# One key projection for two heads of the latent attention, and weight splits over the valid tiles alone

## The chip, the core and the metric

The kernel runs on one core of a Trainium2 chip. The core has a matrix engine (PE, with its own queue for weight loads, PEld), a vector engine (DVE), a scalar engine (ACT), a general engine (POOL) and a sync engine (SP) that issues the loads here. Each engine works through its own instructions in order, and the engines wait for each other by semaphores. The metric is the device time of one execution in microseconds (us), less is better.

## What is computed

Two network blocks run one after the other on 512 tokens of width 1024. The change touches one part of the second block, its latent attention with 8 heads: a query of 64 plain and 32 rotary columns for each head, a key of 64 plain columns for each head, and one rotary key for all heads. In the reference, shortened:

```python
def mla_attention(c_q, c_kv, k_rope_raw, cos, sin, q_norm_g, w_uq, kv_norm_g, w_ukv, w_mla_out):
    q = rms_norm_2(c_q, q_norm_g) @ w_uq                      # 384 -> 8 heads x (64 + 32)
    q_nope, q_rope = q[..., :QK_NOPE], q[..., QK_NOPE:]
    q_rope = apply_rope(q_rope, cos, sin)
    kv = rms_norm_2(c_kv, kv_norm_g) @ w_ukv                  # 256 -> 8 heads x (64 + 64)
    k_nope, v = kv[..., :QK_NOPE], kv[..., QK_NOPE:]
    k_rope = apply_rope(k_rope_raw, cos, sin)
    ...
        s = einsum("bqhd,bkhd->bhqk", qn_b, k_nope) + einsum("bqhr,bkr->bhqk", qr_b, k_rope)
        p = softmax(where(mask, s, neg))
        return einsum("bhqk,bkhd->bqhd", p, v)
```

Beside it stand a convolution of 31 taps with a layer norm, and gates of both branches.

## The kernel before

Every product in full precision is made of three matmuls: a weight is split into a high and a low part (`split`: ACT writes `whi` from `raw`, DVE writes `wlo` as the rest), an input likewise, and high by high, high by low and low by high are summed. Activations are held with features on the 128 partitions and the 512 tokens along the free axis. Weights arrive by units of up to eight 128-column tiles in a ring of four buffers; SP loads a unit into `raw`, ACT and DVE split it three units ahead of its use, and PE's last matmul of a unit counts up `s_used`, which frees the buffer. `split` works on all 1024 columns, also where a unit has fewer.

The latent attention is a loop of 18 steps (`SLOTS`), written out for each engine; the order is the program's, there is no planner. Head h has two steps, 2h and 2h + 1, for two pairs of query blocks. In step s PE does this:

1. the scores of step s (`mla_scores`, L1147 to L1152),
2. a fill unit, 24 matmuls of the input projection (`in_unit`, L774 to L776): into `bank[1]` in even steps, into `bank[0]` in odd ones,
3. the product of probabilities and values of step s - 2 (`mla_pv`),
4. in even steps, the query projection of head s/2 + 1 (`project(h, "q")`, L1128 to L1130, nine matmuls) into `bank[0]`,
5. the transposes of the probabilities of step s - 1 (`mla_turn`, L1166),
6. in even steps, the key projection of the same head (`project(h, "k")`, six matmuls) into `bank[1]`.

A key projection yields 128 rows, 64 of key and 64 of value; the value rows aren't used, since all values are made in a unit of their own before the loop. Head 0 is projected before the loop, its key into `psT`.

The query of head h is taken out of `bank[0]` by two engines: ACT copies the 64 plain rows (L1913), DVE multiplies the 64 rotary rows by the table `rope` (`head_rope`, L2729), both into `tmp[0]`. Then ACT writes the high part `q2h` (L1916) and DVE the low part `q2l` (L2734). The key is split in place: ACT writes `k2h` (L1921), DVE `k2l` (L2740); the rotary key lies in rows 64 to 127 of both buffers already. The fill unit of an odd step waits until both readers of `bank[0]` are done (`h_cp`, `h_rp`); the fill unit of an even step waits for the low part of the key that was in `bank[1]` (`h_lo`).

DVE in step s: the row maxima of the scores (L2834), the split of a fill unit's weights (L2266), the reciprocals (L2850), its share of the convolution taps (L2716, L2721, four in most steps), the eviction of the fill unit (L2690; before the taps in steps 4 and 6), the attention output of step s - 2 (L2877, L2880), in even steps the rope step, the split of a head unit's weights and `q2l`, then the low part of the transposed probabilities (`pt2l`, L2893), and last, in even steps, `k2l`. ACT makes exponentials (L1981) and tap products (L1891) that POOL adds (L3352); POOL also scales the probabilities (L3370). After the taps, step 12 ends with PE's sums for the layer norm (L1116), whose mean DVE takes in step 13 (L2829).

## Time and profile before

| | us |
|---|---|
| median of 3 runs (2504.86 to 2504.95) | 2504.87 |
| profiled execution | 2504.7 |
| its span, first to last instruction | 2502.9 |
| PE busy in the span | 2488.7 (99%) |
| DVE busy | 1991.0 (80%) |
| ACT busy | 1244.7 (50%) |
| POOL busy | 305.5 (12%) |

A row of a timeline gives the start in us from the span's start, the length, engine, line, operation, what is written from what, shapes, and in brackets the idle time of the engine before it with what ended that. PE's matmuls overlap, so their lengths say less than the distances between their starts. A row of the table of waits gives who waited for whom, the total, the number and the longest.

### The profile page before, as it was taken

The page shows a single profiled execution, that of the slowest core. Times are in us where ns is not written, and L with a number is a line of the kernel's source. Part 1 is how long each engine was busy: PE and PEld are TensorE (multiplying, and loading weights), DVE is VectorE, ACT ScalarE, POOL GpSimd, SP SyncE. Part 2 cuts the span into 40 slices and gives each one's busy share as a digit, 9 for nine tenths or more (in the row PEclk, how much of TensorE's full clock was granted, in tenths as well). Part 3 has the DMA queues.
Part 4 walks back from the last instruction along what each step waited for, and adds up shares of the span by engine and source line. Part 5 has one row for each costly group of instructions (what it writes and reads, how often), then busy time and mean ns, then how long its engine had stood idle before and what let it go on. Part 6 is the DMA issues. An engine that isn't in the chain of part 4 may idle for free.

```text
span 2502.9 us, 36450 instructions
## 1 busy us (share of the span) xinstructions
PE 2488.7 (99%) x14212; PEld 2186.1 (87%) x14212; DVE 1991.0 (80%) x2830; ACT 1244.7 (50%) x1975; POOL 305.5 (12%) x250
## 2 busy tenths in 40 slices
PE   9999999999999999999999999999999999999998
PEld 7999988889999889999888899998888888888887
DVE  7878867778888688887777888876899786788873
ACT  6444444444444454444553544445577535654542
POOL 4000001320000000000023100000187221200002
PEclk9999999999999999999999999999999999999999
DMA  5333332223333323334323233334322333233331
GB/s 158 98 96 100 100 104 84 81 86 101 97 105 105 115 83 102 98 101 119 101 61 93 78 104 99 110 103 136 91 71 77 126 92 112 85 106 105 99 100 59
DMA packets 487297, 246.83 MB, mean 99 GB/s; under 512 B 42321, under 2 KB 483926, under 8 KB 486870
## 3 DMA queue, kind: packets, MB, share of 16 engines
q1 hardware_dynamic: 486674, 244.19, 33.9%
q8 instruction: 113, 1.85, 0.3%
q14 instruction: 58, 0.48, 0.1%
q10 hardware_dynamic: 452, 0.32, 0.0%
HBM read 240.27 MB, written 4.19 MB: 98 GB/s over the span
## 4 chain that ended last, share of the span: by engine, by line
PE 96%; DVE 2%; ACT 1%; DMA 0%; issue 0%; POOL 0%; DVEq 0%; ACTq 0%
PE bank L893 8%; PE bank L892 8%; PE bank L891 8%; PE bank L774 6%; PE bank L775 6%; PE bank L776 6%; PE psS L913 5%; PE psS L914 4%; PE psS L915 4%; PE bank L1454 3%; PE psT L957 2%; PE psT L959 2%; PE psT L958 2%; PE psT L774 2%; PE psT L775 2%; PE psT L776 2%
## 5 line engine op out<-in xcount | busy, mean ns | idle before, releaser
L2266 DVE TENSOR_TENSOR wlo<-raw,whi 128x1024 fp32r<-128x1024 f32 (+2 forms) x212 | 288.8, 1364 | 49.2 <-ACT whi L1581 46.0
L774 PE MATMUL bank<-xhl,whi 128*128 128x512 f32 x672 | 264.5, 394 | 0.0
L775 PE MATMUL bank<-xhl,whi 128*128 128x512 f32 x672 | 261.9, 390 | 0.0
L776 PE MATMUL bank<-xhl,wlo 128*128 128x512 f32 x672 | 261.8, 390 | 0.0
L891 PE MATMUL bank<-xshl,whi 128*128 128x256 f32 x840 | 237.8, 283 | 0.0
L892 PE MATMUL bank<-xshl,whi 128*128 128x256 f32 x840 | 237.7, 283 | 0.0
L893 PE MATMUL bank<-xshl,wlo 128*128 128x256 f32 x840 | 237.7, 283 | 0.0
L1581 ACT ACTIVATE whi<-raw 128x1024 fp32r<-128x1024 f32 (+2 forms) x209 | 214.4, 1029 | 37.3 <-PE bank L776 22.0
L2329 DVE TENSOR_TENSOR wlo<-tw,whi 128x1024 fp32r<-128x1024 f32 x140 | 171.6, 1226 | 62.5 <-ACT whi L1621 62.3
L913 PE MATMUL psS<-hhi,whi 128*128 128x512 f32 x488 | 191.7, 393 | 0.0
L914 PE MATMUL psS<-hlo,whi 128*128 128x512 f32 x488 | 191.6, 393 | 0.0
L915 PE MATMUL psS<-hhi,wlo 128*128 128x512 f32 x488 | 189.8, 389 | 0.0
L1621 ACT ACTIVATE whi<-tw 128x1024 fp32r<-128x1024 f32 x140 | 148.1, 1058 | 70.6 <-PE bank L893 56.4
L3258 POOL TENSOR_TENSOR sc<-sc,st 128x1024 f32<-128x1024 f32 (+1 forms) x16 | 27.0, 1685 | 1137.4 <-DVE st L2537 1137.4
L892 PEld LDWEIGHTS bank<-xshl,whi 128*128 128x128 f32 x840 | 161.3, 192 | 0.0
L893 PEld LDWEIGHTS bank<-xshl,wlo 128*128 128x128 f32 x840 | 161.3, 192 | 0.0
L891 PEld LDWEIGHTS bank<-xshl,whi 128*128 128x128 f32 x840 | 161.3, 192 | 0.0
L776 PEld LDWEIGHTS bank<-xhl,wlo 128*128 128x128 f32 x672 | 126.1, 188 | 26.7
L774 PEld LDWEIGHTS bank<-xhl,whi 128*128 128x128 f32 x672 | 126.2, 188 | 26.5 <-issue 1.1
L775 PEld LDWEIGHTS bank<-xhl,whi 128*128 128x128 f32 x672 | 126.3, 188 | 26.1 <-issue 1.0
L1685 ACT ACTIVATE hhi<-tmp 128x512 fp32r<-128x512 f32 x74 | 46.8, 633 | 141.8 <-DVE tmp L2455 138.8
L1628 ACT ACTIVATE whi<-raw 128x384 fp32r<-128x384 f32 (+2 forms) x140 | 79.6, 569 | 74.5 <-PE psS L915 74.1
(703 smaller groups left out, 7184.7 us busy)
## 6 DMA issues: line engine op xcount, KB each, us to landing
raw<-in_ffn_wg SPq DMA_DIRECT2D x88, 512.0 KB
raw<-in_ffn_wu SPq DMA_DIRECT2D x88, 512.0 KB
raw<-in_w_in SPq DMA_DIRECT2D x53, 512.0 KB
raw<-in_w_mlp SPq DMA_DIRECT2D x40, 512.0 KB
raw<-in_ffn_wd SPq DMA_DIRECT2D x48, 256.0 KB
raw<-in_ffn_wd SPq DMA_DIRECT2D x24, 448.0 KB
raw<-in_ffn_wd SPq DMA_DIRECT2D x48, 192.0 KB
raw<-in_ffn_wd SPq DMA_DIRECT2D x48, 128.0 KB
```

The lines of the kernel that those rows point to most:

```text
L774: pe.matmul(dest, a, rhs_hi(k), start=start and k == 0, stop=False)
L775: pe.matmul(dest, a, rhs_lo(k), start=False, stop=False)
L776: mm = pe.matmul(dest, b_, rhs_hi(k), start=False, stop=stop and k == tiles - 1)
L891: pe.matmul(dest, a, mh, start=start and k == 0, stop=False, skip_group_check=resumed)
L892: pe.matmul(dest, a, ml, start=False, stop=False, skip_group_check=resumed)
L893: mm = pe.matmul(dest, b_, mh, start=False, stop=stop and k == 3, skip_group_check=resumed)
L913: pe.matmul(dest, whi[:, a:a + P], chunk(hhi, at_h), start=k == 0, stop=False)
L914: pe.matmul(dest, whi[:, a:a + P], chunk(hlo, at_h), start=False, stop=False)
L915: mm = pe.matmul(dest, wlo[:, a:a + P], chunk(hhi, at_h), start=False, stop=last)
L1581: act.activation(whi[:, a:a + n], raw[:, a:a + n], ACT.Copy).then_inc(s_hi, 1)
L2266: dve.tensor_tensor(wlo[:, a:a + n], raw[:, a:a + n], whi[:, a:a + n].bitcast(F32), ALU.subtract).then_inc(s_split, 1)
L2329: dve.tensor_tensor(wlo[:, a:a + UNIT], tw[:, i * UNIT:(i + 1) * UNIT], whi[:, a:a + UNIT].bitcast(F32), ALU.subtract).then_inc(k_lo, 1)
```

## The change

The weights of the plain keys of heads h and h + 1 (h even) are loaded side by side, so that one key projection yields 64 rows for each of the two. The odd heads' key projections fall away. An odd head's key now lies in rows 64 to 127 of its product, so an odd head keeps plain rows above and rotary rows below: `rope`, the rotary key and the columns of the query weights are laid out to match, for which ACT copies the table once to rows 0 to 63 before the loop. The key of head h + 1 stays in `bank[1]` until step 2h + 1, where ACT and DVE split it after the exponentials, once the scores of the head before in the same buffer are done; the fill unit of the next even step waits for it. Units with 3 or 5 tiles of 128 columns (odd and even heads) are split over 384 or 640 columns. An even head's keys arrive by two transfers, the second with a semaphore of its own (`s_kw`). Some semaphores are renamed and shared with a later stage (left out below).

```diff
+        HEAD_PARTS = [("q", 0), ("k", 0), ("k", 1), ("q", 1)]
+        for h in range(2, H2, 2):
+            HEAD_PARTS += [("q", h), ("k", h), ("k", h + 1), ("q", h + 1)]
+        HEAD_TILES = {C_IN + ORDER.index(("head", h)): QC if h % 2 else QC + KVC for h in range(H2)}
+        def head_part(kind, h):
+            return HEAD_PARTS.index((kind, h)) + 1
+        def head_ready(h):
+            return max(head_part("q", h), head_part("k", h))
+        def head_rows(h):
+            return (slice(NOPE, P), slice(0, NOPE)) if h % 2 else (slice(0, NOPE), slice(NOPE, P))
+        KEY_ROPE_AT = ((NOPE, QK), (0, ROPE))
...
-                    for a, col, n in ((0, i * QK, QK), (QK, r0 + HALF, HALF), (QK + HALF, r0, HALF)):
+                    if i % 2:
+                        parts = ((0, r0, ROPE), (ROPE, r0 + HALF, HALF), (ROPE + HALF, r0, HALF), (NOPE, i * QK, NOPE))
+                    else:
+                        parts = ((0, i * QK, QK), (QK, r0 + HALF, HALF), (QK + HALF, r0, HALF))
+                    for a, col, n in parts:
                         sp.dma_start(dq[:, :, a:a + n], c2(wq, 0, QC, col, n)).then_inc(landed[slot(c)], 16)
-                    sp.dma_start(dk, c2(t["w_ukv_2"], 0, KVC, i * P)).then_inc(landed[slot(c)], 16)
+                    for k in range(0 if i % 2 else KVC):
+                        sp.dma_start(dk[:, k].rearrange("p (h n) -> p h n", h=2), vw[:, k, i:i + 2, 0, :]
+                                     ).then_inc(s_kw if k else landed[slot(c)], 16)
...
             def mla_scores(s):
-                pe.wait_ge(h_lo, 2 * h + 2)
+                pe.wait_ge(h_lo, max(head_ready(h), head_part("k", 1)))
...
-                    elif s // 2 < H2:
-                        pe.wait_ge(h_lo, 2 * (s // 2) + 2)
+                    elif s // 2 < H2 and s // 2 % 2 == 0:
+                        pe.wait_ge(h_lo, head_part("k", s // 2 + 1))
                     else:
                         pe.wait_ge(s_i2, evicted(*FILL[s - 2]))
...
-                if s % 2 == 0 and h < H2:
+                if s % 2 == 0 and h < H2 and h % 2 == 0:
                     pe.wait_ge(s_i2, evicted(*FILL[s]))
                     project(h, "k")
...
             def split(c, q, tiles=8):
+                if HEAD_TILES.get(q + c) == QC + KVC:
+                    act.wait_ge(s_kw, 16 * (sorted(HEAD_TILES).index(c) // 2 + 1))
-                a, n = slot(c) * UNIT, tiles * P
+                a, n = slot(c) * UNIT, HEAD_TILES.get(q + c, tiles) * P
...
             def head_k(h):
-                bb = h % 2 * S
-                act.wait_ge(s_used, unit_of("head", h) + 1)
-                act.activation(k2h[0:NOPE, bb:bb + S], bank_of[("hk", h)][0:NOPE, :], ACT.Copy).then_inc(h_hi, 1)
+                bb, rows = h % 2 * S, head_rows(h)[0]
+                act.wait_ge(s_used, unit_of("head", h - h % 2) + 1)
+                if h >= 2:
+                    act.wait_ge(a_sc, ATT1 + 2 * h - 2)
+                act.activation(k2h[rows, bb:bb + S], bank_of[("hk", h - h % 2)][rows, :], ACT.Copy).then_inc(h_hi, 1)
...
                     e.then_inc(a_ex, 1)
+                if s % 4 == 3 and (s + 3) // 2 < H2:
+                    head_k((s + 3) // 2)
...
                 if s in (4, 6):
                     evict(*FILL[s])
+                if s % 4 == 3 and (s + 3) // 2 < H2:
+                    head_k((s + 3) // 2)
                 if s:
                     taps(DVE_SHARE.get(("slot", s), 0))
...
-                if s % 2 == 0 and h < H2:
+                if s % 2 == 0 and h < H2 and h % 2 == 0:
                     head_k(h)
```

On PE, at the end of step 4 and the start of step 5 (head 3's projections, the transposes of step 3, the scores of step 5). Before:

```order
10729 L1130 MATMUL bank<-lath,wlo 128x512
10730 L1166 MATMUL psT<-ident,p_1_147 128x128 x5
10731 L1128 MATMUL bank<-lath,whi 128x512
10732 L1129 MATMUL bank<-latl,whi 128x512
10733 L1130 MATMUL bank<-lath,wlo 128x512
10734 L1128 MATMUL bank<-lath,whi 128x512
10735 L1129 MATMUL bank<-latl,whi 128x512
10736 L1130 MATMUL bank<-lath,wlo 128x512
10737 L1147 MATMUL psS<-k2h,q2h 128x256
```

And after, with the fill unit of step 5 (L790) at its end:

```order
10723 L1146 MATMUL bank<-lath,wlo 128x512
10724 L1182 MATMUL psT<-ident,p_1_147 128x128 x5
10725 L1163 MATMUL psS<-k2h,q2h 128x256
10726 L1165 MATMUL psS<-maskr,identr 128x128
10727 L1167 MATMUL psS<-k2l,q2h 128x256
10728 L1168 MATMUL psS<-k2h,q2l 128x256
10729 L1163 MATMUL psS<-k2h,q2h 128x384
10730 L1165 MATMUL psS<-maskr,identr 128x128
10731 L1167 MATMUL psS<-k2l,q2h 128x384
10732 L1168 MATMUL psS<-k2h,q2l 128x384
10733 L790 MATMUL bank<-xhl,whi 128x512
```

Six matmuls between the transposes and the scores are gone; the order of the rest is the same.

On DVE, from the rope step of head 2 in step 2 to the taps of step 3 (`tmp_87` is `tmp[0]`, `cw_73` holds the taps). Before:

```order
2051 L2266 TENSOR_TENSOR wlo<-raw,whi 128x1024
2052 L2734 SCALAR_TENSOR_TENSOR q2l<-tmp_87,q2h 128x512
2053 L2893 TENSOR_TENSOR pt2l<-psT,pt2h 128x640
2054 L2740 TENSOR_TENSOR k2l<-bank,k2h 64x512
2055 L2834 TENSOR_REDUCE st_53<-psS 128x1 x2
2056 L2266 TENSOR_TENSOR wlo<-raw,whi 128x1024
2057 L2850 RECIPROCAL st_53<-st_53 128x2
2058 L2721 SCALAR_TENSOR_TENSOR bank<-zpad,cw_73,bank 128x512 x4
```

And after:

```order
2050 L2294 TENSOR_TENSOR wlo<-raw,whi 128x384
2051 L2767 SCALAR_TENSOR_TENSOR q2l<-tmp_87,q2h 128x512
2052 L2929 TENSOR_TENSOR pt2l<-psT,pt2h 128x640
2053 L2773 TENSOR_TENSOR k2l<-bank,k2h 64x512
2054 L2868 TENSOR_REDUCE st_53<-psS 128x1 x2
2055 L2294 TENSOR_TENSOR wlo<-raw,whi 128x1024
2056 L2884 RECIPROCAL st_53<-st_53 128x2
2057 L2773 TENSOR_TENSOR k2l<-bank,k2h 64x512
2058 L2749 SCALAR_TENSOR_TENSOR bank<-zpad,cw_73,bank 128x512 x4
```

The split of head 3's unit shrinks to 384 columns, and the low part of head 3's key comes in between the reciprocals and the taps of step 3; it stood at the end of step 4.

## Rows read from the trace of the kernel before

**Rows 1.** The page: each engine's busy us, share, instructions.

```profile
PE 2488.7 (99%) x14212; PEld 2186.1 (87%) x14212; DVE 1991.0 (80%) x2830; ACT 1244.7 (50%) x1975; POOL 305.5 (12%) x250
```

**Rows 2.** Busy times per engine (x instructions), granted clock, DMA share, GB/s.

```profile
1811.00:1940.00 129.00, 128.97 (x668) 109.02 (x666) 123.12 (x183) 99.63 (x184) 98.71 (x80) 1.00 0.30 76
```

**Rows 3.** Timeline of PE, step 0 to the fill unit of step 1.

```profile
1817.94 0.39 PE L1128 MATMUL bank<-lath,whi 128*128 128x512 f32 x1
...
1821.12 0.39 PE L1130 MATMUL bank<-lath,wlo 128*128 128x512 f32 x1
...
1822.43 0.39 PE L774 MATMUL bank<-xhl,whi 128*128 128x512 f32 x1
```

**Rows 4.** Timeline of DVE in step 0.

```profile
1818.14 0.69 DVE L2688 SCALAR_TENSOR_TENSOR tmp<-bank,inv 128x512 f32<-128x512 f32 x1 [0.75 <-PE bank L776]
...
1820.74 0.69 DVE L2729 TENSOR_TENSOR tmp<-bank,rope 64x512 f32<-64x512 f32 x1
```

**Rows 5.** Timeline of DVE, steps 2 to 4.

```profile
1838.32 0.69 DVE L2729 TENSOR_TENSOR tmp<-bank,rope 64x512 f32<-64x512 f32 x1 [0.54 <-PE bank L1130]
...
1841.42 1.39 DVE L2266 TENSOR_TENSOR wlo<-raw,whi 128x1024 fp32r<-128x1024 f32 x1
...
1848.19 3.10 DVE L2721 SCALAR_TENSOR_TENSOR bank<-zpad,cw,bank 128x512 f32<-128x512 f32 x4
...
1854.24 2.17 DVE L2266 TENSOR_TENSOR wlo<-raw,whi 128x1024 fp32r<-128x1024 f32 x1
...
1860.14 0.69 DVE L2729 TENSOR_TENSOR tmp<-bank,rope 64x512 f32<-64x512 f32 x1
```

**Rows 6.** Timeline of PE, first matmul of step 5's fill unit.

```profile
1860.93 0.47 PE L774 MATMUL bank<-xhl,whi 128*128 128x512 f32 x1
```

**Rows 7.** Timeline of ACT: a key's high part; exponentials ending in steps 3, 7.

```profile
1842.40 0.58 ACT L1921 ACTIVATE k2h<-bank 64x512 fp32r<-64x512 f32 x1
...
1847.72 0.20 ACT L1981 ACTIVATION_READ_ACCUMULATOR p<-psS,st 128x1 f32 x1
...
1885.36 0.20 ACT L1981 ACTIVATION_READ_ACCUMULATOR p<-psS,st 128x1 f32 x1
```

**Rows 8.** Timeline of DVE, steps 6 to 8.

```profile
1874.71 0.67 DVE L2690 TENSOR_TENSOR gate_a<-bank,inv 128x512 f32<-128x512 f32 x1
...
1879.95 1.23 DVE L2266 TENSOR_TENSOR wlo<-raw,whi 128x1024 fp32r<-128x1024 f32 x1
...
1882.92 0.68 DVE L2740 TENSOR_TENSOR k2l<-bank,k2h 64x512 fp32r<-64x512 f32 x1 [0.28 <-ACT k2h L1921]
...
1885.67 3.11 DVE L2721 SCALAR_TENSOR_TENSOR bank<-zpad,cw,bank 128x512 f32<-128x512 f32 x4
...
1891.73 1.67 DVE L2266 TENSOR_TENSOR wlo<-raw,whi 128x1024 fp32r<-128x1024 f32 x1
...
1897.92 0.69 DVE L2729 TENSOR_TENSOR tmp<-bank,rope 64x512 f32<-64x512 f32 x1
```

**Rows 9.** Timeline of PE, fill units: step 6 ends, step 9 starts.

```profile
1874.19 0.39 PE L776 MATMUL bank<-xhl,wlo 128*128 128x512 f32 x1
...
1899.87 0.40 PE L774 MATMUL bank<-xhl,whi 128*128 128x512 f32 x1
```

**Rows 10.** Timeline of POOL in step 4.

```profile
1854.03 1.30 POOL L3352 TENSOR_TENSOR zc<-zc,sqt 128x512 f32<-128x512 f32 x1
```

**Rows 11.** Timeline of DVE, start of step 13.

```profile
1940.40 0.69 DVE L2829 TENSOR_SCALAR var<-bank 128x512 f32<-128x512 f32 x1 [0.36 <-PE bank L1116]
1941.50 0.89 DVE L2834 TENSOR_REDUCE st<-psS 128x1 f32<-128x256 f32 x2 [0.41 <-PE psS L1152]
```

**Rows 12.** Waits of PE, whole span: total us, times, longest us.

```profile
PE bank L1116 <- DVE acc L2843: 0.4, 1, 0.4
```

**Rows 13.** Timeline of SP, issue of a head unit's query weights.

```profile
1803.84 1.43 SPq L698 DMA_DIRECT2D raw<-in_w_uq  x3
```

**Rows 14.** Timeline of ACT, split of a head unit.

```profile
1818.20 1.06 ACT L1581 ACTIVATE whi<-raw 128x1024 fp32r<-128x1024 f32 x1 [2.24 <-PE bank L776]
```

112 lines of the change are left out of this document (59 added, 53 removed).

## The prediction, made before the changed kernel was run

> **What bounds the kernel now.** I read the page first. The line of busy times gives PE 99% of the span and no other engine more than 80% [rows 1], so the time is the length of PE's queue, and a matmul taken out of a stretch without idle time is worth its distance to the next one, not its length. The change lies in the latent attention alone, so next came the busy times of that stretch, about 1811 to 1940 us. There PE is busy for 128.97 of 129.00 us, at the full granted clock, but DVE for 123.12 [rows 2], well over its 80% of the span. The reader is to see two engines that are both nearly full and hand work to each other. PE is the later one nearly everywhere, but DVE has some 6 us of room in 129, and where that room lies decides what a shorter PE queue is worth. So the third view was the timeline of both engines, place by place, to find who waits for whom: where DVE shows idle time before an instruction it has caught up with PE, and where PE's next unit begins right after a DVE step, PE has none left.
>
> **What is removed from PE.** Four key projections go (heads 1, 3, 5, 7), six matmuls each, 24 in all. The projections of step 0 are 15 matmuls from 1817.94 to the start of the last at 1821.12 [rows 3]: 14 distances in 3.18 us, 0.227 each, though one lasts 0.39. So 6 are 1.36 and 24 are 5.44 us. That is the gross gain if nothing else comes late, 0.217% of 2504.87. Everything below asks how much of it other engines take back.
>
> **What is added and moved.** The weights of six of the head units that are split inside the loop shrink from 1024 columns to 384 or 640. A split of 1024 by DVE takes 1.23 alone [rows 8], a 512-column step 0.68 (the low part of a key, same rows), so by that slope 384 columns take 0.54 and 640 take 0.82: 0.69 or 0.41 saved, more where the split was stretched. ACT saves as much in proportion, but it is not the late engine. The low part of an odd head's key keeps its price of 0.68 and moves from the end of an even step to the middle of the odd step before it, ahead of the convolution taps. There DVE must also wait for ACT: in step 3 the exponentials end at 1847.92 (1847.72 and 0.20), the high part of the key takes 0.58, so DVE can begin its part at about 1848.45 and the taps at 1849.02 instead of 1848.19, 0.83 later [rows 5, 7]. In step 7 the exponentials end at 1885.56 and the taps begin at 1885.67; by the same steps they would begin at about 1886.66, 0.99 later [rows 7, 8]. So what the smaller splits save is about what the move costs DVE between one odd head and the next, while PE wants to be 1.36 faster each time. The copy of the rotary table on ACT (one 64x512 step, 0.58 like the key's), the extra SP issue for an even head and the first head's second key all lie before step 0, where the scores wait for none of them; I price them at nothing, and at 0.6 if that cover were gone. The renamed semaphores count the same events.
>
> **The four places.** The removed matmuls stood between the query projection of an odd head and the fill unit of the next step. That unit writes the bank from which DVE's rope step (L2729) still reads that query, so it waits for the rope step (and for ACT's copy of the other rows, which ends earlier). This cover is what goes.
>
> (a) Steps 0 to 1. DVE's chain starts when PE ends the fill unit (1818.14, after 0.75 of waiting for PE), so it can't move, and its rope step ends at 1821.43 [rows 4]. PE began the unit at 1822.43 [rows 3] and would be ready at 1821.07. In step 4 PE began 0.10 after the end of the rope step (1860.83, 1860.93) [rows 5, 6], so here it begins at 1821.53: 0.46 of the 1.36 is lost, **0.90 stays** (0.62 if the scores of step 2 then wait for their exponentials, 1.00 without the 0.10).
>
> (b) Steps 2 to 5. At 1838.32 DVE has just waited 0.54 for PE's query of head 2: both are level. From there to the rope step of head 3 (1860.14, end 1860.83) DVE has no idle time, and PE begins its unit 0.10 later [rows 5, 6]. PE has no room at all here. In this stretch DVE gets back 0.69 to 0.85 from the split of 384 columns (it was 1.39 long) and gives 0.83 for the moved key, so it arrives when it did. **0.06 of 1.36 stays.** The two long splits set the bounds: 2.17 at 1854.24 against 1.23 alone. If that stretching went, 0.9 more would stay; with a little more of it, minus 0.1.
>
> (c) Steps 6 to 9. DVE could run ahead after (b), but its eviction of the fill unit of step 6 began at 1874.71, and PE's last matmul ended at 1874.58 [rows 8, 9], so no more than 0.09 can be gained before it. After that the split of head 5 saves 0.69, and the next key step (1882.92) waited 0.28 for ACT already, so the saving becomes more waiting there. The moved key of head 5 costs 0.99. The rope step ended at 1898.61 (1897.92 and 0.69) [rows 8], and would end at 1899.51; with 0.10, PE starts at 1899.61 where it could at 1898.51 (1899.87 less 1.36) [rows 9]: 1.10 lost, **0.26 stays**. The split at 1891.73 took 1.67 against 1.23 alone, so 0.70 may stay, or minus 0.07.
>
> Rows show what stretches these splits. The one at 1854.24 ends at 1856.41, and POOL's add that began before it (1854.03) ends at 1855.33, 1.08 before that, which is about a whole lone split [rows 5, 10]; the lone 1.23 is from a time without a POOL add. The Trainium skill, page "SBUF — State Buffer", section "Who interferes with whom", says that a DVE instruction with two SBUF inputs and a GpSimd one that reads SBUF take turns, the first holding the way for its whole length. The trace agrees with 1855.33 and 1856.41. By that rule the split in (c), which would then begin just after an add, waits for all of it and nothing stays there, 1.8 in all; by the mean of the row lengths it is 0.26 and 2.0. I keep the rows.
>
> (d) Steps 12 to 14. Here no rope step is near; PE's sums for the layer norm just start 1.36 earlier. DVE takes their result at 1940.40 after a wait of 0.36, and the maxima of step 13 at 1941.50 after 0.41 [rows 11]. From those DVE runs through to the sum of squares for which PE is seen to wait (0.4) [rows 12], so PE gains what DVE gains at the maxima. DVE was ready at 1940.04; the moved key of head 7 adds about 0.9, its old place gives back 0.68, so 1940.26, and the maxima follow 0.6 later at 1940.9 instead of 1941.5. That is 0.6, and up to 1.2 if a split in step 12 is less stretched: **0.8 stays** (0.3 to 1.2).
>
> **The sum.** 0.90 + 0.06 + 0.26 + 0.80 = 2.0 us of 5.44. Only two waits at the program's start stand above this 0.4 in the list of PE's waits [rows 12], so a gain is kept to the end. The profiled execution took 2504.7 (span 2502.9 and 1.8 around it), the median is 2504.87; the same 2.0 off the median is 2502.8.
>
> **Rivals.** *All of it.* If DVE's stretched steps (0.9 in (b), 0.4 in (c), more in step 2) vanish since shorter splits leave POOL and DVE fewer meetings, DVE keeps pace and 5.44 plus the 0.1 that PE loses at 1860.93 would come: 2499.4. For it: DVE's own work does fall. Against it: (a) holds by PE's own time, and DVE's slack is nil at 1860. 0.05.
>
> *Nothing of it.* DVE is the bound from step 2 to 14, (c) and (d) give nothing, and a late exponential in step 1 takes (a) down to 0.6: about 2504.3. For it: DVE has 95% in the stretch. Against it: DVE waits for PE at 1838.32 and 1940.40 and is level with it at 1874.71. 0.13.
>
> *Slower, by late weights.* The keys of an even head now come as two transfers with pieces of 256 bytes where 512 stood, and ACT waits for both. In the nearest rows the issue is at 1803.84 and ACT's split of that unit at 1818.20 [rows 13, 14], 14.4 us. It decides only when a landing needs more than that; at 16.7 us for each of three units it costs 7 us, 2509.8 after the gain. Nothing in the rows comes near, since pieces of 64 bytes are in these units already. The Trainium skill, page "DMA: Bandwidth & Descriptors", section "Specifications", asks for 512 bytes or more for line rate, which speaks against this piece of the change; no run here shows the price yet. 0.02.
>
> **How the numbers follow.** The forecast has 0.80, all of it, nothing and slower the rest. Adding the bounds of the four places gives 1.00 + 0.96 + 0.70 + 1.2 = 3.9 at best and 0.62 - 0.1 - 0.07 + 0.3 = 0.75 at worst, so 2501.0 to 2504.1; towards the full gain and towards nothing I open it to 2500.7 and 2504.3. A measurement of this kernel can tell 0.2%, 5.0 us, from no change. Faster by more needs nearly the whole gross: 0.04. Slower by more: 0.03. Within: 0.93.
>
> **What would show it.** The three matmul lines of the projections would show 32 instructions each where 40 stood. The fill unit of step 1 would begin about 0.1 after the end of head 1's rope step, and so in steps 5 and 9, with idle PE before it of about 0.5, 1.3 and 1.1, put down to DVE's rope step; DVE would show its moved key step waiting for ACT in steps 3, 7 and 11. I am wrong if PE has no idle time in the stretch (then all of it came), if the waits fall on ACT's copy of the query or on POOL, or if PE waits for a split of weights (late loads).

## The result and the profile after

The changed kernel takes **2510.05 us** (median of 15 runs, 2508.39 to 2510.59) where the kernel before took 2504.97 (15 runs, 2504.69 to 2505.19): a ratio of 1.0019 with the interval [1.0011, 1.0026]. It is 5.1 us slower, 0.20%, where 2.0 us less was forecast and the range ended at 2504.3. Its times fall into two groups, seven at 2508.4 to 2509.1 and eight at 2510.05 to 2510.6. The profiled execution is of the lower group: 2508.91, span 2507.1, so 4.2 more than the 2504.7 of the kernel before.

In the page's busy times PE loses 24 matmuls and 2.8 us, DVE's sum is what it was [rows 1]:

```profile
PE 2485.9 (99%) x14188; PEld 2182.3 (87%) x14188; DVE 1991.0 (79%) x2830; ACT 1242.6 (50%) x1976; POOL 301.7 (12%) x250
```

The busy times of the changed stretch (window, length, then PE, PEld, DVE, ACT, POOL with instructions, granted clock, DMA share, GB/s) answer to [rows 2]:

```profile
1811.00:1940.00 129.00, 123.40 (x641) 104.00 (x641) 119.41 (x179) 95.00 (x180) 96.31 (x80) 1.00 0.31 74
```

PE was busy for 128.97 of these 129 us and now is for 123.40. So 5.6 us of idle time stand where 5.44 us of matmuls were taken out, and none of it shows as a shorter program. The waits of PE from 1800 to 1970 us (what waits, what released it; total us, times, longest; those above 0.2) show where:

```profile
PE bank L790 <- issue: 4.3, 2, 2.8
PE bank L1132 <- DVE acc L2877: 2.0, 1, 2.0
PE psS L1163 <- ACT p L2007: 0.6, 1, 0.6
PE bank L790 <- ACT tmp L1935: 0.4, 1, 0.4
```

Before, the only one of these was 0.4 on L1116, the sum of squares [rows 12], which is L1132 now. The timeline of PE at these places (start, length, the wait before in brackets):

```profile
1821.90 0.47 PE L790 MATMUL bank<-xhl,whi 128*128 128x512 f32 x1 [0.37 <-ACT tmp L1935]
...
1828.74 0.30 PE L1163 MATMUL psS<-k2h,q2h 128*128 128x128 f32 x1 [0.59 <-ACT p L2007]
...
1862.51 0.47 PE L790 MATMUL bank<-xhl,whi 128*128 128x512 f32 x1 [2.75 <-issue]
...
1901.77 0.47 PE L790 MATMUL bank<-xhl,whi 128*128 128x512 f32 x1 [1.56 <-issue]
...
1956.27 1.82 PE L1132 MATMUL bank<-tmp,ones 128*128 128x512 f32 x2 [2.02 <-DVE acc L2877]
...
1958.81 1.36 PE L790 MATMUL bank<-xhl,whi 128*128 128x512 f32 x1
```

And DVE's steps that these wait for, from the timeline of DVE (columns as above):

```profile
1838.73 0.69 DVE L2762 TENSOR_TENSOR tmp<-bank,rope 64x512 f32<-64x512 f32 x1 [0.22 <-PE bank L1146]
...
1841.83 1.04 DVE L2294 TENSOR_TENSOR wlo<-raw,whi 128x384 fp32r<-128x384 f32 x1
...
1848.62 0.69 DVE L2773 TENSOR_TENSOR k2l<-bank,k2h 64x512 fp32r<-64x512 f32 x1 [0.31 <-ACT k2h L1945]
1849.35 3.13 DVE L2749 SCALAR_TENSOR_TENSOR bank<-zpad,cw,bank 128x512 f32<-128x512 f32 x4
...
1855.56 2.32 DVE L2294 TENSOR_TENSOR wlo<-raw,whi 128x1024 fp32r<-128x1024 f32 x1
...
1861.72 0.68 DVE L2762 TENSOR_TENSOR tmp<-bank,rope 64x512 f32<-64x512 f32 x1
...
1866.00 2.31 DVE L2294 TENSOR_TENSOR wlo<-raw,whi 128x1024 fp32r<-128x1024 f32 x1 [0.55 <-ACT whi L1599]
...
1884.42 0.68 DVE L2773 TENSOR_TENSOR k2l<-bank,k2h 64x512 fp32r<-64x512 f32 x1 [0.74 <-ACT k2h L1945]
...
1887.71 0.69 DVE L2773 TENSOR_TENSOR k2l<-bank,k2h 64x512 fp32r<-64x512 f32 x1 [0.45 <-ACT k2h L1945]
...
1894.64 1.70 DVE L2294 TENSOR_TENSOR wlo<-raw,whi 128x1024 fp32r<-128x1024 f32 x1
...
1900.98 0.68 DVE L2762 TENSOR_TENSOR tmp<-bank,rope 64x512 f32<-64x512 f32 x1
...
1944.11 0.87 DVE L2868 TENSOR_REDUCE st<-psS 128x1 f32<-128x256 f32 x2
1944.91 1.74 DVE L2294 TENSOR_TENSOR wlo<-raw,whi 128x1024 fp32r<-128x1024 f32 x1
```

PE's two long waits, 2.75 and 1.56, are put down to "issue", that is to nothing seen. But the rope step of head 3 ends at 1862.40 and PE starts at 1862.51; that of head 5 ends at 1901.66 and PE starts at 1901.77. These are waits for DVE: PE starts 0.11 after its step, as it did in [rows 5, 6]. The label is to be distrusted there, and the runs below bear that out. The wait of 0.37 before the unit of step 1, put down to ACT's copy of the query, is of the same kind: ACT's copy ended at 1821.71, DVE's rope step at 1821.80, PE starts at 1821.90.

How much later than before PE stands at each place, and what each stretch adds beside what was forecast for it:

| stretch, up to | PE later than before, us | added in it | forecast |
|---|---|---|---|
| before step 0 (1811.5) | +0.30 | +0.30 | 0 |
| fill unit of step 1 | -0.53 | -0.83 | (a) -0.90 |
| scores of step 2 | +0.37 | +0.90 | 0 |
| fill unit of step 5 | +1.58 | +1.21 | (b) -0.06 |
| fill unit of step 9 | +1.90 | +0.32 | (c) -0.26 |
| scores of step 12 | +2.34 | +0.44 | 0 |
| scores of step 13 | +1.43 | -0.91 | (d) -0.80 |
| sum of squares, step 14 | +3.10 | +1.67 | 0 |
| 1961.86, behind it | +4.82 | +1.72 | 0 |
| end of the span | +4.2 | -0.6 | 0 |

The 0.30 ahead of the loop stands already at the first projection of a head (1797.23, before 1796.94), and where it comes from was not followed; the output transfers at the end are 0.6 shorter. The 0.44 before step 12 is mostly a key projection in step 10, which starts at 1919.04, behind DVE's eviction that ends at 1918.98. What is left to explain are the stretches to step 2, to step 5 and to step 14, and the 1.72 behind it. That one is TensorE's clock. The busy times in 2 us windows there (columns as before, the granted clock behind POOL's busy time):

```profile
1956.00:1958.00 2.00, 1.73 (x3) 0.75 (x4) 0.21 (x1) 1.46 (x3) 0.00 (x0) 0.64 0.00 0
1958.00:1960.00 2.00, 2.00 (x4) 0.90 (x3) 0.17 (x1) 0.00 (x0) 0.00 (x0) 0.51 0.00 0
1960.00:1962.00 2.00, 2.00 (x11) 1.64 (x10) 2.00 (x4) 1.42 (x2) 0.19 (x1) 1.00 0.00 0
```

PE waits 2.02 for DVE, and as it starts again the granted clock is 0.64 and then 0.51, the lower of its two levels (1.2 GHz). The four matmuls of the sums and the nine behind them take 2.54 and 3.05 us where they took 1.42 and 2.45: 1.12 + 0.60 = 1.72.

### The profile page after: what moved, and what is told of

Same layout as the page of the kernel before. It is cut to its first block, busy times and chain, and to the rows that moved or that the text cites. A ratio compares the mean times of both kernels' runs of the same rounds, so it can differ in the third digit from the quotient of the medians.

```text
span 2507.1 us, 36413 instructions
## 1 busy us (share of the span) xinstructions
PE 2485.9 (99%) x14188; PEld 2182.3 (87%) x14188; DVE 1991.0 (79%) x2830; ACT 1242.6 (50%) x1976; POOL 301.7 (12%) x250
## 4 chain that ended last, share of the span: by engine, by line
PE 91%; DVE 5%; ACT 2%; issue 1%; POOL 0%; DMA 0%; DVEq 0%; ACTq 0%; POOLq 0%
PE bank L909 8%; PE bank L908 8%; PE bank L907 8%; PE bank L790 5%; PE bank L792 5%; PE bank L791 5%; PE psS L929 4%; PE psS L930 4%; PE psS L931 4%; PE bank L1470 3%; PE psT L973 2%; PE psT L974 2%; PE psT L975 2%; PE psT L790 1%; PE psT L792 1%; PE psT L791 1%
## 5 line engine op out<-in xcount | busy, mean ns | idle before, releaser
L2294 DVE TENSOR_TENSOR wlo<-raw,whi 128x1024 fp32r<-128x1024 f32 (+3 forms) x212 | 287.5, 1358 | 52.3 <-ACT whi L1599 49.2
L790 PE MATMUL bank<-xhl,whi 128*128 128x512 f32 x672 | 265.5, 395 | 4.7 <-issue 4.3
L1599 ACT ACTIVATE whi<-raw 128x1024 fp32r<-128x1024 f32 (+4 forms) x209 | 211.0, 1013 | 36.3 <-PE bank L792 19.9
L790 PEld LDWEIGHTS bank<-xhl,whi 128*128 128x128 f32 x672 | 126.4, 188 | 32.1 <-issue 6.1
```

Source lines behind the costliest of these rows:

```text
L790: pe.matmul(dest, a, rhs_hi(k), start=start and k == 0, stop=False)
L1599: act.activation(whi[:, a:a + n], raw[:, a:a + n], ACT.Copy).then_inc(s_hi, 1)
L2294: dve.tensor_tensor(wlo[:, a:a + n], raw[:, a:a + n], whi[:, a:a + n].bitcast(F32), ALU.subtract).then_inc(s_split, 1)
```

## The experiments

The theory (D where the quoted texts use a letter) was that DVE is the pace of steps 2 to 14: the move costs it more than the smaller splits give, so PE waits, and that the waits bring the clock down. Sixteen kernels were run, each in five rounds beside the kernel before, which had medians of 2504.8 to 2505.0 in every batch.

### Which part of the change costs

The moved step stands in steps 3, 7 and 11 (the section on the change says step 2h + 1 for head h + 1; by its diff it is 2h - 1). It is taken out on both engines (e1), and on DVE alone (e2). In both DVE loses:

```diff
 # DVE's program, inside the loop over steps; in e1 ACT's program too
-                if s % 4 == 3 and (s + 3) // 2 < H2:
-                    head_k((s + 3) // 2)
                 if s:
                     taps(
```

> The changed kernel without the moved key step of heads 3, 5 and 7, on ACT and on DVE (these heads then use the plain key rows of head 1, so that part of the computation is left out). Theory D (DVE's chain of work from step 2 to step 14 is the bound, and the moved key step made it longer by 1.16, 1.26 and 1.28 us in steps 3, 7 and 11): DVE's rope step of head 3 ends at about 1861.2 instead of 1862.40, PE's fill unit of step 5 follows 0.1 behind, PE has no wait of 2.0 before the sum of squares near 1956 and keeps its full clock there; 2503 us (2501.5 to 2504.5). Rival I (the idle time before the fill units of steps 5 and 9, which the list of waits puts to PE's own issue, is a hold-up of PE's instruction stream): the idle time stays, 2508 to 2510. Rival C (what was lost is the clock alone, for a reason outside the attention loop): 2508 or more.

> The changed kernel without DVE's half of the moved key step of heads 3, 5 and 7; ACT's half stays (the low parts of these keys are left out of the computation). Theory D: nearly the same as without the whole step, as DVE then goes from the reciprocal straight to the taps; ACT's 0.6 in steps 3, 7 and 11 costs at most 0.3 each where DVE waits for ACT's next split; 2503.5 us (2502 to 2505). Rival A (ACT's chain, which the same step lengthened by 0.6 to 0.8, is the bound, and DVE only follows it): 2507 to 2509.

Measured: e1 **2503.11** (2502.75 to 2503.38), ratio 0.9993 [0.9984, 1.0002]; e2 **2503.03** (2502.8 to 2503.22), 0.9993 [0.9984, 1.0001]. So the three moved steps cost the changed kernel 7 us, and it is DVE's half alone that costs them; ACT's half is free. Not all of this is waiting: between the profiled executions (2508.91 and 2503.01) 1.7 of the 5.9 us is the clock at the sum of squares, which stays at 1.00 in e1 and e2, where that wait is 1.4. In the timeline of DVE of e2 the taps of step 3 and the rope step of head 3 stand 1.36 and 1.69 earlier than in the changed kernel (0.23 of each stood before the loop):

```profile
1847.99 3.11 DVE L2755 SCALAR_TENSOR_TENSOR bank<-zpad,cw,bank 128x512 f32<-128x512 f32 x4
...
1860.03 0.68 DVE L2768 TENSOR_TENSOR tmp<-bank,rope 64x512 f32<-64x512 f32 x1
```

And in its waits of PE (1800 to 2000) the 4.7 before the fill units (4.3 for "issue", 0.4 for ACT's copy) have shrunk to 1.9, though nothing but a DVE step was taken away:

```profile
PE bank L795 <- ACT tmp L1941: 1.7, 2, 1.3
...
PE bank L795 <- issue: 0.2, 1, 0.2
```

The wait of 1.3 is put down to ACT's copy of the query, but that ended at 1859.87, DVE's rope step at 1860.71, and PE starts at 1860.81. Even with that step gone DVE's rope step of head 3 is only 0.11 ahead of the 1860.14 of before [rows 5], with 1.36 us of matmuls less on PE and a smaller split on DVE. That is the first sign that DVE's timetable set the pace already.

Next, the splits alone: in the changed kernel they go back to 1024 columns (e4).

```diff
-                a, n = slot(c) * UNIT, HEAD_TILES.get(q + c, tiles) * P
+                a, n = slot(c) * UNIT, tiles * P
```

> The changed kernel with the weights of the head units split over 1024 columns again, on ACT and DVE. Theory D: the narrower splits do relieve DVE, by 0.35 to 1.0 each and partly lost again in waiting for ACT, so without them DVE is later still: 2511 (2509.5 to 2513). Rival M (the narrower splits shift DVE's steps so that later splits meet POOL's adds and last longer, 2.31 instead of 1.51 in step 4 and 2.30 instead of 1.37 in step 8; this eats all that they save, or more): 2508 to 2509.5.

Measured: **2511.92** (2510.37 to 2512.1), ratio 1.0026 [1.0017, 1.0036]. The smaller splits are worth 1.9 (e4's times have two groups too, and like groups are 1.7 to 1.8 apart), not the 3.3 that the prediction's prices, 0.69 and 0.41 for three steps each, sum to. In the timeline of DVE the split of step 2 is here

```profile
1842.88 1.74 DVE L2294 TENSOR_TENSOR wlo<-raw,whi 128x1024 fp32r<-128x1024 f32 x1
```

against 1.04 for 384 columns above and 1.39 for 1024 before [rows 5]. The length of a split depends as much on when it meets POOL's add as on its columns: the add that began ahead of each ends 1.09 before the end of the split in e4 (1843.53, 1844.62), 1.07 before (1841.74, 1842.81) and, with 384 columns, 0.41 (1842.46, 1842.87).

Third, the sum of squares. In the changed kernel it comes behind all 24 matmuls of its fill unit instead of after the first 15 of them (e3), so PE has work during the wait.

```diff
-                in_unit(*FILL[s], ready=(lambda k: conv_square_sums() if k == 5 else None) if s == LN_VAR + 1 else None)
+                in_unit(*FILL[s])
+                if s == LN_VAR + 1:
+                    conv_square_sums()
```

> The changed kernel with the two matmuls of the layer norm's sum of squares behind all 24 matmuls of the fill unit of step 14, not behind the first 15. The last 9 (2.04 us) then cover the wait of 2.02 before them. Theory D with the clock as its consequence (PE fell to 1.2 GHz after 2 us without work): no wait, granted clock 1.00 throughout, 3.7 us less than the profiled run of the changed kernel, 2505.2 (2504.4 to 2506.5), and the times form one group. Rival (the lower clock there does not come from the wait): only the wait goes, 2506.9 or more, and 1956 to 1960 still shows a clock of about 0.5.

Measured: **2507.91** (2506.35 to 2509.26), ratio 1.0011 [1.0003, 1.002]. It gives 2.1, not the 3.7 expected, and its times don't form one group. In its profile the wait at the sum is gone and the clock there is 1.00 from 1954 to 1964, so the lower clock at that place did come with the wait; 0.5 comes back as a wait for DVE in step 15. But this profiled execution, 2509.26, is the longest of its runs, and shows the clock falling at another place. The first matmul of step 5's unit in the timeline of PE, and the busy times behind it:

```profile
1862.32 0.77 PE L790 MATMUL bank<-xhl,whi 128*128 128x512 f32 x1 [2.75 <-issue]
```

```profile
1862.00:1864.00 2.00, 1.68 (x4) 1.42 (x5) 1.97 (x4) 1.72 (x3) 0.00 (x0) 0.50 0.00 1
1864.00:1866.00 2.00, 2.00 (x6) 1.52 (x6) 1.46 (x4) 2.00 (x4) 1.55 (x2) 0.50 0.98 244
1866.00:1868.00 2.00, 2.00 (x6) 1.53 (x5) 2.00 (x1) 2.00 (x6) 1.86 (x2) 0.50 0.06 17
```

The same wait of 2.75 stood in the changed kernel's profile at a clock of 1.00, and here is followed by six us at 0.50, with 6 matmuls in 2 us where 9 fit at full clock. From the first matmul of the unit to the scores of step 6 it is 9.56 us here and 6.68 there, 2.9 lost. So one kernel can meet the same wait with and without the fall.

### Was DVE the pace before?

Two kernels change the kernel before. e5 gives PE alone the relief: the second projection of each pair is one matmul in place of six, 20 fewer in all, and the odd heads' keys are not computed. e6 gives DVE and ACT alone the relief: smaller splits, here 640 columns for every head.

```diff
 # e5, in the projection
+                if part == "k" and h % 2:
+                    pe.matmul(dest, wcols(wlo, c, k0), chunk(lath, l0), start=True, stop=True).then_inc(s_used, 1)
+                    return
 # e6, in both split routines
-                a, n = slot(c) * UNIT, tiles * P
+                a, n = slot(c) * UNIT, HEAD_TILES.get(q + c, tiles) * P
```

> The kernel before with one matmul in place of six in the key projections of heads 1, 3, 5 and 7 (20 matmuls, 4.5 us of PE's queue, so these keys are not computed); all else, DVE's and ACT's steps among it, as before. This is what PE's part of the change does alone. Theory D: DVE's rope step of head 3 still ends at about 1860.8, PE waits some 1.2 us for it and DVE's chain then sets the pace, so little over half of the 4.5 comes: 2503.0 (2502.2 to 2504.2). Rival S (a shorter PE queue is itself what costs time: PE waits, its clock falls, and the time rises): 2506 or more. Rival F (DVE follows a faster PE everywhere): 2500.4.

> The kernel before with the head units split over the 640 valid columns in place of 1024, on ACT and DVE; nothing else. Theory D: before, PE is the later engine nearly everywhere (0.4 us of waiting in the loop), so the time DVE saves, 0.4 for each of seven heads, shows as idle time of DVE: 2504.6 (2504.2 to 2505.0). Rival M (the narrower splits shift DVE against POOL and this costs by itself): over 2505.2.

Measured: e5 **2504.57** (six runs at 2504.2 to 2504.6, five at 2505.95 to 2506.3), ratio 1.0001 [0.9992, 1.001]; e6 **2504.49** (2504.32 to 2504.74), 0.9999 [0.999, 1.0008]. Twenty matmuls, 4.5 us at 0.227, are worth nothing that can be told from no change (0.2). This is the plainest result of the study. In the timeline of DVE of e5:

```profile
1838.27 0.70 DVE L2732 TENSOR_TENSOR tmp<-bank,rope 64x512 f32<-64x512 f32 x1 [0.36 <-PE bank L1133]
...
1860.26 0.69 DVE L2732 TENSOR_TENSOR tmp<-bank,rope 64x512 f32<-64x512 f32 x1
...
1898.02 0.69 DVE L2732 TENSOR_TENSOR tmp<-bank,rope 64x512 f32<-64x512 f32 x1
...
1940.07 0.67 DVE L2832 TENSOR_SCALAR var<-bank 128x512 f32<-128x512 f32 x1
```

These four stood at 1838.32, 1860.14, 1897.92 and 1940.40 [rows 5, 8, 11]. With PE relieved of up to 4.5 us, DVE's timetable moves by no more than 0.12 until step 9, and by 0.33 until step 13. What PE gained became waits, in its timeline (the first again ends 0.10 after DVE's rope step, 1860.95, and not with ACT's copy, 1860.40):

```profile
1861.05 0.47 PE L774 MATMUL bank<-xhl,whi 128*128 128x512 f32 x1 [1.08 <-ACT tmp L1916]
...
1952.84 1.12 PE L1116 MATMUL bank<-tmp,ones 128*128 128x512 f32 x2 [1.94 <-DVE acc L2846]
```

The expectation by D, 2503.0, was missed as well: more of PE's gain was lost than the theory had it. (e5's upper group is where rival S stood, 2506; its profile is of the lower one and shows no lower clock.) Relief of DVE and ACT alone (e6) is worth no more, 0.3, which can't be told from no change either; in its timeline of DVE the rope step of head 2 waits for PE for 0.98, where it waited 0.54 [rows 5].

```profile
1838.30 0.69 DVE L2731 TENSOR_TENSOR tmp<-bank,rope 64x512 f32<-64x512 f32 x1 [0.98 <-PE bank L1132]
```

By this the two engines were level before the change, and only a change that relieves both could pay. Both together (x1) were the test of that:

> The kernel before with both single edits together: one matmul in place of six in the key projections of heads 1, 3, 5 and 7 (these keys are not computed), and the head units split over 640 columns. By themselves they gave 0.2 and 0.3. D2 (DVE and PE were level before, so neither pays alone): together they give clearly more than 0.5, 2503.0 (2502.3 to 2503.8). Rival (DVE alone was the limit, or ACT or POOL is one too): the sum of the two, 2504.3, or no more than either.

Measured: **2505.13** (five runs at 2503.3 to 2504.0, six at 2505.1 to 2505.4), ratio 0.9998 [0.9989, 1.0007]. The 2503.0 expected was missed, and the median is no better than with either edit alone, as the rival had it. The profiled execution is of the upper group, and its busy times show the fall of the clock at the sum of squares:

```profile
1952.00:1954.00 2.00, 2.00 (x3) 0.95 (x4) 0.00 (x0) 1.18 (x1) 0.00 (x0) 0.60 0.00 0
1954.00:1956.00 2.00, 2.00 (x5) 1.02 (x4) 0.58 (x1) 0.00 (x0) 0.00 (x0) 0.55 0.00 0
```

Here 4.5 us less on PE and some 2.9 less on DVE (seven splits at the prediction's 0.41) came to 1.2 at the sum of squares (1951.97, before 1953.17), and behind it PE is 0.5 later than before: the upper group loses even that. So PE and DVE are not the whole limit. What a split saves turns into a longer wait of the next low key for ACT (0.28 before [rows 8]); in the timelines of ACT and DVE of x1

```profile
1879.21 0.63 ACT L1921 ACTIVATE q2h<-tmp 128x512 fp32r<-128x512 f32 x1 [1.70 <-DVE tmp L2734]
...
1882.17 0.68 DVE L2745 TENSOR_TENSOR k2l<-bank,k2h 64x512 fp32r<-64x512 f32 x1 [0.68 <-ACT k2h L1926]
```

Between the rope step and the low key ACT works without idle time, 2.9 us from the start of the query's high part to the end of the key's (1882.13), and DVE's split lies beside this work. There a shorter split can't bring the low key forward.

### Can another engine take DVE's step?

POOL has 12% of busy time over the span [rows 1]. In v1 it takes the low part of the odd keys: ACT also copies the plain key to `tmp[1]`, and POOL subtracts. v2 adds e3's edit.

```diff
 # POOL's program, steps 3, 7, 11
+                    pool.tensor_tensor(k2l[rows, S:2 * S], tmp[1][rows, :], k2h[rows, S:2 * S].bitcast(F32),
+                                       ALU.subtract).then_inc(s_kp, 1)
 # ACT's program
+                    act.activation(tmp[1][rows, :], bank_of[("hk", (s + 1) // 2)][rows, :], ACT.Copy).then_inc(s_kc, 1)
```

> The changed kernel with DVE's half of the moved key step (heads 3, 5, 7) given to POOL: ACT copies the key rows once more, unrounded, to a free SBUF tile (0.58 behind its high part), and POOL subtracts there, behind its scaling of the probabilities; the computation is complete. Theory D: as with DVE's half left out, 2503.2 (2502.4 to 2504.4), no lower clock. Rival P (POOL's extra step, two SBUF inputs, makes DVE's steps longer by as much as was taken from it, or ACT's second copy makes the splits late): 2505 to 2508.

> As the one before, and the sum of squares behind the whole fill unit of step 14, where 9 matmuls (2.04 us) cover PE's wait (1.4 us without DVE's half of the key step). Theory D: 1.4 less again, 2501.9 (2501.0 to 2503.0), which would be less than both kernels. Rival (DVE's steps behind the sum then come 0.6 us later and PE waits for them in step 15 or 16): no less than the one before.

Measured: v1 **2511.28** (2507.95 to 2512.32), ratio 1.0023 [1.0014, 1.0031]; v2 **2508.99** (2507.74 to 2510.51), 1.0017 [1.0009, 1.0026]. D was wrong here and its rival P right in kind, though both times lie above its range as well: POOL is not free within the stretch. POOL's subtraction, in its timeline:

```profile
1849.99 1.30 POOL L3427 TENSOR_TENSOR k2l<-tmp,k2h 64x512 fp32r<-64x512 f32 x1 [0.46 <-ACT acc L1919]
```

Its sums of products then come later, so ACT, which writes the products into two buffers, waits for them twice, in the timeline of ACT:

```profile
1852.70 0.73 ACT L1919 ACTIVATE acc<-zpad,cw 128x512 f32<-128x512 f32 x1 [0.99 <-POOL zc L3400]
...
1854.14 0.72 ACT L1919 ACTIVATE sqt<-zpad,cw 128x512 f32<-128x512 f32 x1 [0.71 <-POOL zc L3400]
```

and ACT's split of the next weights, which stands behind these, reaches DVE late (timeline of DVE):

```profile
1855.84 2.22 DVE L2308 TENSOR_TENSOR wlo<-raw,whi 128x1024 fp32r<-128x1024 f32 x1 [1.73 <-ACT whi L1609]
```

The step that was taken from DVE came back as 1.73 of waiting, and PE's wait before the unit of step 5 is the longest of the study. It is put down to ACT's copy, which ended at 1861.74, but ends 0.10 after DVE's rope step, at 1862.59 (timelines of DVE and PE):

```profile
1861.91 0.68 DVE L2776 TENSOR_TENSOR tmp<-bank,rope 64x512 f32<-64x512 f32 x1
...
1862.69 0.69 PE L797 MATMUL bank<-xhl,whi 128*128 128x512 f32 x1 [3.21 <-ACT tmp L1945]
```

POOL's busy time would have told: in this stretch it is 98.71 of 129 us [rows 2], 77% and not 12%.

### Orders of the same work

w1: ACT splits the next weights ahead of the trailing products in steps 0, 4, 8 and 12 (and no longer at the start of the step after), against DVE's waits of 0.55 for `whi`. w2: the odd head's key step stands right behind the even one's, on ACT and DVE, outside the stretch between two taps. w3 has both, w4 both and e3's edit.

```diff
 # w1, ACT's program
+                if s % 4 == 0 and h < H2:
+                    split(unit_of(*FILL[s + 1]) + AHEAD, 0)
                 products(share - (3 * some if s else 1))
 # w2, ACT's and DVE's programs; the step in s % 4 == 3 goes
                 if s % 2 == 0 and h < H2 and h % 2 == 0:
                     head_k(h)
+                    head_k(h + 1)
```

> The changed kernel with ACT's split of the next fill unit's weights ahead of its last convolution products in steps 0, 4, 8 and 12 (there the key step no longer stands between). The runs so far left this theory, D2: from step 1 to step 12 DVE's own timetable sets the pace, in the kernel before too, and what the narrower splits and the missing key step free on DVE in steps 4 and 8 is lost because its next split then waits for ACT's (2.09 us in step 1, 0.55 in steps 4 and 8) and lands on POOL's adds. D2: those waits go, DVE is 0.5 earlier from step 5 and 1.0 from step 9 on, the scores of step 2 come 0.6 earlier; 2507.4 (2506.3 to 2508.8). Rival P2 (ACT's products, now later, hold up POOL's adds and through them ACT itself, as the kernel with POOL's extra step showed): no faster than the changed kernel, 2509 to 2511.

> The changed kernel with the key step of heads 3, 5 and 7 right behind that of heads 2, 4 and 6, on ACT and on DVE, not behind the exponentials of the odd step. D2: DVE then pays 0.6 to 0.7 for it without a wait for ACT (0.31, 0.44 and 0.45 before), 0.5 less each time, and the row maxima come 0.6 later, for which PE has room in steps 7 and 11 (the scores of the next step begin 1.5 after the last exponential) but not in step 3; 2507.5 (2506.0 to 2509.0). Rival (the place makes no difference, only the amount of work on DVE does): 2509 to 2510.3.

> Both edits of the two before together. D2: their gains add up, since both shorten the same chain, 2505.9 (2504.6 to 2507.5). Rival (they free the same idle time): no faster than the better of the two.

> As the one before, with the sum of squares behind the whole fill unit of step 14. D2: PE's wait there (1.4 to 2.0) is covered, 1.4 less, 2504.5 (2503.2 to 2506.2). Rival (the wait moves to DVE's next step): no faster than the one before.

| kernel | median (lowest to highest), us | ratio to before |
|---|---|---|
| w1 | 2507.49 (2507.26 to 2509.39) | 1.0013 [1.0003, 1.0022] |
| w2 | 2505.56 (2505.38 to 2507.27) | 1.0006 [0.9997, 1.0014] |
| w3 | 2507.13 (2506.87 to 2508.91) | 1.0011 [1.0003, 1.002] |
| w4 | 2506.35 (2506.15 to 2506.54) | 1.0006 [0.9997, 1.0015] |

w2 gives back 4.5 of the 5.1 us: two adjacent low keys wait for ACT once, and the taps don't wait. In its timeline of DVE

```profile
1845.30 1.40 DVE L2772 TENSOR_TENSOR k2l<-bank,k2h 64x512 fp32r<-64x512 f32 x2
...
1883.67 1.41 DVE L2772 TENSOR_TENSOR k2l<-bank,k2h 64x512 fp32r<-64x512 f32 x2 [0.74 <-ACT k2h L1945]
```

the first pair waits for nothing. So most of the cost was the place of the step, not the step. Part of the 4.5 is the clock: w2's profile, of its lower group, shows 1.00 behind the same wait of 2.02, and like groups of the two kernels are 3.1 to 3.4 apart. Its time lies below the range expected of it (2506.0 to 2509.0). w1's 2.6 and w2's 4.5 don't add (w3 gives 2.9). In w1 the wait for `whi` goes, but one for ACT's exponentials comes in, two us further on (timeline of DVE):

```profile
1866.77 0.17 DVE L2887 RECIPROCAL st<-st 128x2 f32<-128x2 f32 x1 [0.72 <-ACT p L2008]
```

ACT cannot do one thing earlier without doing another later. That holds for w3 as well, 1.6 above w2: the scores of step 2 wait 1.24 for exponentials where they wait 0.57 in w2, and the key projection of step 10 waits 0.81 for DVE's eviction, in w2 not at all. So w3 met its rival, no faster than the better of the two, and w4, with 0.8 less than w3, missed its 2504.5.

Last, e3's edit on w2 (x2); or, on w2 (x3) and on the kernel before (x4), DVE's Newton steps of the first normalization, 5 us in step 13 ahead of the acc that the sum of squares waits for, put behind the second merge unit (the counters that change places with it are left out):

```diff
-                if s == LN_VAR:
-                    newton(FIRSTN, first_inv, inv6)
 # behind the merge's low part
+                if m == 1:
+                    newton(FIRSTN, first_inv, inv6)
```

> The changed kernel with the odd heads' key step behind the even heads' (the best version so far, 2505.5) and the sum of squares behind the whole fill unit of step 14. D2: the wait of 2.02 is covered; of its 2.0 some 0.5 to 1.2 comes back as a wait in step 15 (as with both other edits, where 0.75 stayed); one group of times, 2504.6 (2504.0 to 2505.2). Rival: nothing stays, 2505.5.

> The changed kernel with the odd heads' key step behind the even heads', and the Newton steps of the first norm (5 us on DVE in step 13, needed only by the last sums of this block) moved behind the second merge unit; the sum of squares stays where it was. D2: DVE reaches the sum's additions up to 5 us earlier, PE's wait of 2.02 goes and with it the lower clock; one group of times, 2503.5 (2502.8 to 2504.5), less than both kernels. Rival (POOL's and ACT's part of the layer norm, not DVE's, sets that wait, or the moved steps hold up the merge): 2505 or more.

> The kernel before with the same move of the Newton steps, nothing else. D2: only the wait of 0.35 for the sum goes, 2504.5 (2504.1 to 2504.9). Rival (the move is worth more by itself, so x3's gain is not the change's): 2503.8 or less.

| kernel | median (lowest to highest), us | ratio to before |
|---|---|---|
| x2 | 2504.76 (2504.53 to 2504.95) | 0.9999 [0.9991, 1.0008] |
| x3 | 2504.32 (2503.91 to 2504.61) | 0.9997 [0.9988, 1.0006] |
| x4 | 2504.24 (2503.94 to 2504.36) | 0.9997 [0.9988, 1.0006] |

x2 and x3 take the changed kernel back to the time before. x4, without the change, is as good as x3: 0.7 below the 2504.97 (2504.51 to 2505.17) of its batch, with no overlap of the times, though the interval of the ratio holds 1. In x3 a wait of PE for the same acc is left, 0.9, and in x4 none is. No kernel here shows a gain from the removed matmuls beyond e1 and e2, which leave the moved step or DVE's half of it out, and their 1.9 us is below what this measurement tells from no change.

## Why the prediction was wrong

**The premise.** "DVE has some 6 us of room in 129" was read as room that PE's shorter queue could use. e5 shows there was none: with 4.5 us less on PE, DVE's timetable moved by 0.33. Of the 5.9 us in [rows 2], the trace of before has 1.9 as DVE's waits for ACT and 1.3 as waits for PE; the rest lies in gaps that the list of waits doesn't show. The two instants at which DVE waited for PE, 0.54 and 0.36 [rows 5, 11], meant that it was level, and were read rightly as that; what was not drawn from it is that then the change has to be judged as a change of the chain that runs through DVE and ACT, with PE's 5.44 as an upper bound.

**(b) and (c): the step that failed** is "what the smaller splits save is about what the move costs DVE". By it DVE's rope step of head 3 "arrives when it did"; it came 1.58 later (1861.72, 1860.14). Costs: the key step was priced at 0.83 and 0.99 of delay. It waits 0.31, 0.45 and 0.45 for ACT, takes 0.69 to 0.70, and puts the taps of step 3 at 1849.35, 1.16 later than 1848.19. Gains: the split of 384 columns was to save 0.69 to 0.85 and saved 0.35 (1.04 against 1.39), beside a POOL add. In step 6 what the split saved turned into a longer wait of the next key for ACT (0.74 against 0.28). In steps 4 and 8 DVE, ahead by the low key that had gone, ran into ACT's `whi`: it waited 0.55, and then its split met POOL's add and took 2.31. The prediction said for (c) that a saving "becomes more waiting there", and did not carry the thought to the other places.

Nor did it carry the delay. Each place was worked out from DVE's old timetable, but DVE never got back to it: it is 1.58 later than before at the rope step of head 3, 3.06 at that of head 5 (1900.98, 1897.92) and 2.61 at the maxima of step 13 (1944.11, 1941.50).

The Trainium skill's rule of the page "SBUF — State Buffer", section "Who interferes with whom", by which a DVE step with two inputs in SBUF and a POOL step that reads SBUF take turns, had been set aside for a mean of row lengths. The trace agrees with it again. In the changed kernel 1024 columns took 2.32 and 2.31, where 1.23 is the lone price [rows 8], and the POOL add that began ahead of each ends 1.09 before the split does (timeline of POOL, for the split at 1855.56; the last section counts the others):

```profile
1855.50 1.29 POOL L3388 TENSOR_TENSOR zc<-zc,acc 128x512 f32<-128x512 f32 x1
```

For (c), though, it would not have helped: there both engines came later alike, and the split took 1.70 (1894.64) where it had taken 1.67 [rows 8]. The 0.32 that the table shows there came from DVE's delay, not from this split.

**(a)** held at its own place, 0.83 of 0.90, and was lost one step on. The 0.62 that the bound kept became -0.07, since the scores of step 2 wait 0.59 for exponentials. No row stood behind the 0.62: those exponentials ended at 1828.03, 0.34 ahead of the scores of step 2 (1828.37), so more than that could stay only if they came earlier too. They ended 0.57 later, at 1828.60. Behind that is a tap on ACT that waited for POOL, in the timelines of ACT of the changed kernel and of the kernel before:

```profile
1825.16 0.73 ACT L1909 ACTIVATE sqt<-zpad,cw 128x512 f32<-128x512 f32 x1 [2.09 <-POOL zc L3388]
```

```profile
1824.15 0.72 ACT L1891 ACTIVATE sqt<-zpad,cw 128x512 f32<-128x512 f32 x1 [1.44 <-POOL zc L3352]
```

PE came earlier, POOL 1.01 later.

**(d)** came near by its number alone: PE gains 0.91 at the scores of step 13 where 0.80 was to stay. It was priced on DVE's maxima, 0.6 earlier than 1941.50, and these came 2.61 later. The prediction then said that DVE "runs through to the sum of squares" and that the gain is kept. DVE did run through, with its delay, and its split in front of it took 1.74 at 1944.91 where 1.23 stood. PE waits 2.02 there, so all of PE's gain at step 13 and more, 1.67 in all, is lost at step 14.

**The clock** had no term. 1.72 us of the 4.2 in the profile are matmuls at the lower level after PE's wait of 2.02. No row of the kernel before could show it, since its longest wait in the stretch was 0.4; but the prediction's own idle times of 0.5, 1.3 and 1.1 on PE were put at their length and no more. At that length it would have been right: in no profile here did a lower clock follow a wait of 1.43 or less.

**The rivals.** "Nothing of it" was nearest in its condition, DVE as the bound of steps 2 to 14, though its 2504.3 is 5.75 too low; its 0.13 was too little. "All of it" fell (by its own terms it sums to 2499.3). The slower rival fell too, though its 2509.8 is close to the 2510.05 measured: that is chance. No wait of PE or ACT for a landing appears in the stretch, so the pieces of 256 bytes cost nothing seen here, and a price of theirs no run shows; ACT's split of [rows 14] begins at 1818.49, 0.29 later than before where PE is 0.30 later. The Trainium skill, page "DMA: Bandwidth & Descriptors", section "Specifications", asks for 512 bytes or more for line rate. The slower outcome came by a mechanism that was in the text, the moved step, with a price on the wrong side of nought, and by the clock. Slower by more than 5.0 had been given 0.03.

**The signs.** Three came as foretold: 32 instructions on each projection line for 40, the fill units of steps 1, 5 and 9 starting 0.10 to 0.11 after the rope steps, and DVE's key step waiting for ACT in steps 3, 7 and 11. The idle times did not: 0.37, 2.75 and 1.56 for 0.5, 1.3 and 1.1, and the list puts none of them to DVE's rope step. So that PE would wait for these rope steps was right; how late DVE would be, and what that does at step 14, was not.

**Open.** Which stretch makes the upper group of the changed kernel's times, some 1.3 us above the lower, was not seen, since the profile is of a lower one; that the clock falls at step 5's unit there and not at the sum, as in the profile of e4's upper group (2.9 lost as in e3 in place of 1.7, 1.2 apart), is argued and not shown.

## What to carry to other kernels

Where one engine is 99% busy and another, in the stretch, 95%, and the rows show each waiting now and then for the other, they are level: taking work from one was worth nothing here (e5, e6), and from both little (x1), since the chain ran through a third. The change must be priced on the chain of the others, the steps it moves first, and a delay there is carried on from place to place. A step that must wait for another engine costs more ahead of a long step with no slack than beside a step that waits for the same thing anyway (w2: 4.5 of 5.1 us back, 3.1 to 3.4 between like groups). And busy shares are to be taken in the stretch, for the helpers too: POOL had 12% of the span and three quarters of this stretch, and one step more there came back as waiting (v1).
